# Both feed-forward products of a hybrid decoder step recast as seven block products, with the hidden activations passed through DRAM

## The reference

```python
x = x + mix
xn = rmsnorm(x, p['norm2_w'])
hid = jnp.square(jax.nn.relu(xn @ p['w_up']))     # 1024 -> 4096
x = x + hid @ p['w_down']                         # 4096 -> 1024
...
y = rmsnorm(x, final_norm_w)
```

## Time and profile before

| what | us |
|---|---|
| median of 3 runs | 2190.42 (2189.12 to 2192.53) |
| profiled execution, its span | 2187.7 |
| TensorE busy in the span | 2161.0 (99%) |
| VectorE, ScalarE, GpSimd busy | 972.0, 758.3, 570.4 |

### The profile page before, as it was taken

How to read it: one execution, slowest core, us unless ns; L and a number is a source line. 1 busy time by engine, 2 the same in 40 slices (tenths; PEclk the granted TensorE clock), 3 DMA queues, 4 the chain that set the end, 5 groups by cost and what they waited for, 6 DMA issues and landing times.

```text
span 2187.7 us, 36227 instructions
## 1 busy us (share of the span) xinstructions
PE 2161.0 (99%) x13766; PEld 2100.4 (96%) x13766; DVE 972.0 (44%) x1524; ACT 758.3 (35%) x1344; POOL 570.4 (26%) x375
## 2 busy tenths in 40 slices
PE   7999999999999999999999999999999999999998
PEld 6999999999899999899998999999999999999998
DVE  5888332334666563244445466442222222222226
ACT  5556323233456463233332334241212213122132
POOL 2338623233121112212213222222121222212120
PEclk9999999999999999999999999999999999999999
DMA  4224546442244323446432743211111111111112
GB/s 171 71 84 132 170 128 178 140 123 83 80 127 144 121 78 126 140 145 192 146 117 62 242 158 138 98 29 59 30 58 38 43 54 32 58 34 53 53 39 89
DMA packets 191538, 222.09 MB, mean 102 GB/s; under 512 B 38670, under 2 KB 146226, under 8 KB 191334
## 3 DMA queue, kind: packets, MB, share of 16 engines
q1 hardware_dynamic: 164364, 179.81, 27.1%
q10 hardware_dynamic: 27098, 41.23, 5.3%
HBM read 162.22 MB, written 58.77 MB: 101 GB/s over the span
## 4 chain that ended last, share of the span: by engine, by line
PE 77%; issue 10%; POOL 5%; DVE 4%; DMA 2%; ACT 1%; SPq 1%; ACTq 0%; POOLq 0%; DVEq 0%
PE D L438 64%; POOL w_lo L418 2%; PE D L2854 2%; POOL b_t L744 1%; POOL b_u L741 1%; DVE u_x L552 1%; DMA w_raw<-in_w_half 1%; PE MM L1906 1%; DMA d_bc<-rowd 0%; PE MB L1990 0%; PE MM L878 0%; PE MB L2302 0%; PE D L2397 0%; PE MB L2251 0%; PE MB L2270 0%
## 5 line engine op out<-in xcount | busy, mean ns | idle before, releaser
L438 PE MATMUL D<-xn_hi,w_hi 128*128 128x352 f32 x1992 | 661.9, 332 | 1.8 <-ACT u_in L513 1.0
L418 POOL TENSOR_TENSOR w_lo<-w_raw,w_hi 128x1024 fp32r<-128x1024 f32 (+1 forms) x163 | 339.1, 2080 | 1173.3 <-ACT w_hi L412 1173.3
L438 PE MATMUL D<-xn_lo,w_hi 128*128 128x352 f32 x1992 | 642.7, 323 | 0.0
L438 PE MATMUL D<-xn_hi,w_lo 128*128 128x352 f32 x1992 | 642.5, 323 | 0.0
L438 PEld LDWEIGHTS D<-xn_hi,w_hi 128*128 128x128 f32 x1992 | 374.5, 188 | 16.3 <-issue 12.8
L438 PEld LDWEIGHTS D<-xn_lo,w_hi 128*128 128x128 f32 x1992 | 374.5, 188 | 4.7 <-issue 3.8
L438 PEld LDWEIGHTS D<-xn_hi,w_lo 128*128 128x128 f32 x1992 | 374.3, 188 | 0.0
L412 ACT ACTIVATE w_hi<-w_raw 128x1024 fp32r<-128x1024 f32 (+1 forms) x163 | 143.8, 882 | 346.7 <-PE D L438 295.2
L438 PE MATMUL D<-z_lo,w_hi 128*128 128x352 f32 x768 | 247.9, 323 | 0.0
L438 PE MATMUL D<-z_hi,w_lo 128*128 128x352 f32 x768 | 247.8, 323 | 0.0
L438 PE MATMUL D<-z_hi,w_hi 128*128 128x352 f32 x768 | 247.3, 322 | 0.0
(11 more groups left out here) (565 smaller groups left out, 3063.6 us busy)
## 6 DMA issues: line engine op xcount, KB each, us to landing
w_raw<-in_w_proj SPq DMA_DIRECT2D x73, 512.0 KB, 3.9
proj<-stage ACTq DMA_DIRECT2D x60, 528.0 KB, 3.1
w_raw<-in_w_half SPq DMA_DIRECT2D x72, 256.0 KB, 2.6
w_raw<-in_w_full SPq DMA_DIRECT2D x24, 512.0 KB, 3.6
stage<-proj SPq DMA_DIRECT2D x23, 528.0 KB, 3.5
d_bc<-rowd SPq DMA_DIRECT2D x32, 256.0 KB, 5.6
m_in<-proj SPq DMA_DIRECT2D x32, 256.0 KB, 3.9
f_w<-in_w_full SPq DMA_DIRECT2D x16, 512.0 KB, 3.6
```

Source lines behind the costliest of these rows:

```text
L418: nc.gpsimd.tensor_tensor(w_lo[t.slot][:, 0:kt, :], raw(t)[0][:, 0:kt * P].rearrange("p (k m) -> p k m", m=P), w_hi[t.slot][:, 0:kt, :].bi ...
L438: last = nc.tensor.matmul(D[b][:, 0:GN], w[t.slot][:, k, :], x, start=(k == 0 and n == 0), stop=(k == kt - 1 and n == 2))
```

## The change

Both products are made in 2 x 2 blocks. For an up product the two halves of the output rows (a pair of tiles), the two halves of the inner dimension (even and odd k-tiles) and the two quarters of a column half (QW = 264) form the blocks; a scheme of 7 block products (i = 0 to 6) instead of 8 gives the four output blocks. A *round* is one pair of output tiles over a list of k-pairs `ks`. It has 7 products, each for both column halves n, each with 3 matmuls of 264 columns per k-pair. There are 16 up rounds over 4 k-pairs (2688 matmuls), then 20 down rounds (`DOWN_ROUNDS`) and 4 last ones (`LAST_ROUNDS`), together 64 k-pair steps (2688 matmuls).

Sums of weight blocks are made by GpSimd (4 per round, between 7 low parts), the high parts by ScalarE; a ring of 8 slots holds the parts, so the weights of product i of round s + 1 can be made once product i - 1 of round s is done. The seven classes of the input (3 plain blocks and 4 differences) are made for z in `out_proj` and for the hidden tiles in the down rounds listed in `PREPARED`, always one k-pair per round: ScalarE rounds, VectorE makes 7 low parts and 4 differences of 528 columns. `W_STEPS` below is GpSimd's order in a round: l is a low part, s a block sum that ScalarE's high part waits for.

Hidden tiles are stored to DRAM (`hd`) by SyncE after their squares, and loaded again for the down phase. Four tiles of `acc` are parked in DRAM (`resid`) meanwhile. All loops of this part are unrolled. Shortened to what the text behind speaks of:

```diff
-FB = 8
-FT = D_FF // P // FB
+QW = T // 4
+NCLS = 7
+UPS = D_FF // P // 2
+RING = 8
...
+        def room(pe, s, i, n):
+            s0, i0 = {0: (s - 2, 6), 1: (s - 1, 5), 2: (s, 0), 3: (s - 1, 3), 4: (s, 2), 5: (s, 1), 6: (s, 4)}[i]
+            if s0 >= 0:
+                pe.wait_ge(*(read_act if s0 < DOWN0 and i0 < 3 else read_dve)(s0, i0, n))
...
+        def product(pe, s, i, n):
+            up, pair, ks = ROUNDS[s]
+            pe.wait_ge(*w_made(s, f"l{i}"))
+            if up:
+                if s == 0:
+                    pe.wait_ge(*n2_dve.after(f"l{i}3"))
+            else:
+                pe.wait_ge(x_low, L_AT[ks[-1], i])
+            room(pe, s, i, n)
...
+            for k, kp in enumerate(ks):
+                xh, xl = x_hi[kp % 4][:, i, n, :], x_lo[kp % 4][:, i, n, :]
+                for j, (w, x) in enumerate(((hi, xh), (hi, xl), (lo, xh))):
+                    last = pe.matmul(to, w[:, k, :], x, start=fresh and k == 0 and j == 0, stop=k == len(ks) - 1 and j == 2, skip_group_check=True)
...
+        W_STEPS = ["l0", "s1", "l1", "s2", "l2", "s4", "l3", "s5", "l4", "l5", "l6"]
...
+        def w_high(act, s, i):
+            act.wait_ge(fw_ld[s % 2], 32 * (s // 2 + 1))
+            if i in (1, 2, 4, 5):
+                act.wait_ge(*w_made(s, f"s{i}"))
...
+        def up_copy(act, s, i):
+            for n in range(2):
+                act.wait_ge(*done(s, i, n))
+                if s:
+                    act.wait_ge(h_st[OUT_AT[i][0]][n], 16 * s)
+                elif i == 0:
+                    act.wait_ge(*n2_dve.after(f"a{KT - 1}"))
+                act.activation(hid(n, i), bank8(bank_of(s, i, n)), ACT.Copy).then_inc(f_act, 1)
...
+        def down_add(dve, s, i, n):
+            dve.wait_ge(*done(s, i, n))
+            dve.tensor_tensor(to, to, bank8(bank_of(s, i, n)), ALU.add).then_inc(f_dve, 1)
...
+        def feed_sp(sp):
+            w_load(sp, 0)
+            park(sp, 0)
+            w_load(sp, 1)
+            park(sp, 1)
+            for s in range(DOWN0):
+                if s >= 1:
+                    w_load(sp, s + 1)
+                if s == DOWN0 - 2:
+                    x_load(sp, 0)
+                    x_load(sp, 1)
+                for t in range(2):
+                    for n in range(2):
+                        sp.wait_ge(f_sq, 8 * s + 4 + 2 * t + n + 1)
+                        sp.dma_start(hd[2 * s + t, :, half(n)], stage[:, n, t * 2 * QW:(t + 1) * 2 * QW]).then_inc(h_st[t][n], 16)
+            for s in range(DOWN0, N_ROUNDS):
+                if s + 1 < N_ROUNDS:
+                    w_load(sp, s + 1)
+                if s == DOWN0:
+                    unpark(sp, 1)
+                    unpark(sp, 0)
+                for kp in X_LOADS.get(s - DOWN0, ()):
+                    x_load(sp, kp)
...
+        def feed_act(act):
...
+            for s in range(1, DOWN0):
+                for i in range(NCLS):
+                    if i < 3:
+                        up_copy(act, s, i)
+                    if i == 0:
+                        up_square(act, s - 1, NCLS - 1)
+                    if i >= 4:
+                        up_square(act, s, {4: 3, 5: 4, 6: 5}[i])
+                    if s == DOWN0 - 1:
+                        for kp in range(2):
+                            x_split_high(act, kp, i)
+                    w_high(act, s + 1, i)
+            up_square(act, DOWN0 - 1, NCLS - 1)
+            for s in range(DOWN0, LAST0):
+                for i in range(NCLS):
+                    if s - DOWN0 in PREPARED:
+                        x_split_high(act, PREPARED[s - DOWN0], i)
+                    w_high(act, s + 1, i)
...
+        def feed_dve(dve):
...
+            for s in range(DOWN0, LAST0):
+                for i in range(NCLS):
+                    for n in range(2):
+                        down_add(dve, s, i, n)
+                    if s - DOWN0 in PREPARED:
+                        x_split_low(dve, PREPARED[s - DOWN0], i)
```

More of the change, by code:

```diff
@@ new lines, in build @@
+        Round = namedtuple("Round", "up pair ks")
+        UP_ROUNDS = [Round(True, m, range(4)) for m in range(UPS)]
+        DOWN_ROUNDS = [Round(False, 1, range(0, 1)), Round(False, 2, range(0, 2))]
+        for first in range(0, 15, 3):
+            DOWN_ROUNDS += [Round(False, 0, range(first, first + 3)), Round(False, 3, range(first, first + 3))]
+            if first < 12:
+                DOWN_ROUNDS += [Round(False, 1, range(first + 1, first + 4)), Round(False, 2, range(first + 2, first + 5))]
@@ new lines, in build @@
+        X_AT = {x: k + 1 for k, x in enumerate(X_ORDER)}
+        X_STEPS = [step for kp, i in X_ORDER for step in [("low", kp, i)] + ([("difference", kp, NEXT_DIFFERENCE[i])] if i in NEXT_DIFFERENCE else [])]
+        L_AT = {(kp, i): k + 1 for k, (what, kp, i) in enumerate(X_STEPS) if what == "low"}
+        T_AT = {(kp, i): k + 1 for k, (what, kp, i) in enumerate(X_STEPS) if what == "difference"}
+        fw_ld = [sem(f"fw_ld{s}") for s in range(2)]
+        fw_high, fw_pool, fp_done = sem("fw_high"), sem("fw_pool"), sem("fp_done")
@@ new lines, in z_total, with z_roots @@
+        def z_total(pe):
+            pe.wait_ge(*n2_dve.after(f"a{KT - 1}"))
+            for lo, hi, b in SUM_COLS:
+                last = pe.matmul(bank8(b, hi - lo), ones, RS2[:, lo:hi], start=True, stop=True)
+            last.then_inc(*n2_pe.step("z"))
+        def z_roots(act):
+            act.wait_ge(*n2_pe.after("z"))
+            for g in (2, 0, 1):
+                lo, hi, b = SUM_COLS[g]
+                act.activation(RS2[:, lo:hi], bank8(b, hi - lo), ACT.Ln, bias=EPS, scale=1.0 / D_MODEL).then_inc(*n2_act.step(f"l{g}"))
+                act.wait_ge(*n2_act.after(f"l{g}"))
+                act.activation(RS2[:, lo:hi], RS2[:, lo:hi], ACT.Exp, scale=-0.5).then_inc(*n2_act.step(f"r{g}"))
@@ new lines, in feed_pe @@
+        def feed_pe(pe):
+            for s in range(LAST0):
+                for i in range(NCLS):
+                    for n in range(2):
+                        product(pe, s, i, n)
+                    if s == 0 and i == 2:
+                        z_total(pe)
+            for n in range(2):
+                for s in range(LAST0, N_ROUNDS):
+                    for i in range(NCLS):
+                        product(pe, s, i, n)
+                    if n and s == LAST0:
+                        last_total(pe, 0)
+            last_total(pe, 1)
@@ L3287 @@
     half = [tiles(wb[b], 4) for b in (HG, GD, ML)]
-    down = a["w_down"][0].reshape(FB, FT * P, D_MODEL)
-    half += [tiles(down[f], FT) for f in range(FB)]
     w_half = np.concatenate(half, 0)
```

728 lines of the change are left out of this document (462 added, 266 removed).

## The result

The changed kernel takes 2265.89 us (median of 4 runs, 2265.35 to 2266.86) against 2190.18 us (4 runs): ratio 1.0345, 95% interval 1.033 to 1.0359. It is slower by 3.4%, where 2197 (2150 to 2235) was forecast. The likeliest case had the sign, but the time lies outside the range. The profiled execution has a span of 2263.5 us against 2187.7.

A forecast was written before the change was run, and what follows sets the result against it. TensorE, busy in 99% of the span, was taken as the bound; -74.7 us for matmuls against added waits, start, handover and tail summed to +6.6, span 2194.3, forecast 2197 us, range 2150 to 2235.

The forecast's parts named there:

- The likeliest case: Whole kernel: the forecast itself, slower at 2197 us, own range 2180 to 2212, chance 0.40.
- the up rounds' term: 14 up rounds: late weight load delays ScalarE, GpSimd and the copy TensorE needs before product 4; +39 us (20 to 60).
- the loop: Up rounds: load, high parts with GpSimd's steps, squares, store and copies, without TensorE, take 23.5 us a round.
- The handover: Rounds 16 to 18: VectorE late, round 18's weights queued behind 4.3 MB; 39 us instead of 31, +8.5 (4 to 20).
- Start: Round 0 waits on input parts, copies and high parts, +10 us (6 to 16); VectorE and GpSimd in `out_proj`, +3.
- Last rounds: Rounds 21 to 23: GpSimd makes weights while TensorE needs them at once, +4.4; products with ones cost 1.4.
- B: Matmuls: 264 columns take 112.5 ns, only down and last rounds gain, 28 us, so 2169; chance 0.10.
- D: Matmuls: the distance stays 159.7 ns despite fewer columns, some 2360 us; chance 0.05.
- The matmuls' term: Feed-forward part: 5376 matmuls of 264 columns at 123 ns make 661.2 us, -74.7 us.
- prepared rounds: Down rounds: VectorE's two-SBUF-tile operations and GpSimd's exclude each other, TensorE waits 1.2 and 1.8 us; +12 us (0 to 45).
- rival C: Down phase: shared SBUF access sets the pace, 38 us instead of 12, so 2223; chance 0.20.
- Rival A: Up rounds: TensorE stays the bound because the load's landing hides, so 2158 us; chance 0.25.

The follow-up runs named there:

- experiment 2: Changed kernel with 24 matmuls whose result nobody reads added before product 4 of rounds 1 to 14; 2255.86 us, ratio 1.0293.
- experiment 9: Changed kernel, load still late, with ScalarE's copies of products 1 and 2 ahead of the next weights' high parts in rounds 1 to 14; 2249.76 us.
- experiment 5: On top of experiment 1: round 0's high parts ahead of the copies, three high parts of round 1 after that round's first copy; 2184.37 us.
- Experiment 3: Changed kernel with GpSimd's 11 operations in rounds 17 to 35 covering only the first 128 of 384 columns; 2248.72 us, ratio 1.026.
- experiment 1: Changed kernel with the up weights of round s + 2 loaded in round s, ahead of its stores; 2189.16 us, ratio 0.9994.
- experiment 10: Changed kernel with early loads and reordered start, handover and tail (2177.33 us), plus copies of products 1 and 2 ahead of high parts; 2201.45 us.

## Why the prediction was wrong, and where it was right

**The step that failed is the up rounds' term, +39, which measured +73.0.** The mechanism was the forecast one, a late load that comes round to TensorE through ScalarE and GpSimd. Two sizes in it were wrong. The first and larger is the loop. It was put at 23.5 us a round and takes 25.0 in experiment 2, where hardly a matmul runs at the lower clock, and 24.7 in experiment 9, where the waits stand elsewhere. Most of the difference lies between high part 5 and the next load: squares, stores, their landing, copies and squares again take 5.8 us for 4.6. The up rounds of experiment 2, its filler counted as waiting, come to 63.0 us of the 73.0, so 24 of the 34 us that the term is off are the loop's.

The second is an assumption that stood nowhere as a term: that a waiting TensorE goes on at the distance of 123 ns when the wait ends. The earlier trace rows show a clock of 1.00, but in a stretch without a pause, so they say nothing of a kernel with one. After ten of the 14 pauses matmuls ran at a clock of 0.50 for 3 to 6 us, which costs 1.5 to 2.6 us each. In these rounds it is 20.0 us on 51.9 of pauses, in the whole feed-forward part some 30. Experiment 2 shows the cause: with the pause filled, 1.5 of the 20.0 are left. It shows the price as well, the other 10 us, since a faster TensorE waits longer for the same loop. The Trainium skill describes this (TensorE: Matmul & The Clock Gate, "HAM oscillation — how this bites in real kernels"): a kernel whose matmuls wait for a transfer in each tile starts again at half clock each time. The trace agrees for ten of the 14 pauses, with 11 matmuls in 2 us for 18, and not for the other four. That section was the one to weigh against this change, and the prediction didn't.

**The handover, +8.5, measured +22.9**, over its upper bound of 20. The forecast counted the lag of VectorE and the queue, and both are there: SyncE's issues in order of time in the changed kernel, then ScalarE, VectorE and TensorE:

```profile
1870.60 0.94 SPq L2910 DMA_DIRECT2D raw<-in_w_dn  x2
1871.59 2.19 SPq L3181 DMA_DIRECT2D acc<-resid  x4
1874.02 1.52 SPq L3072 DMA_DIRECT2D f_rs<-hd  x2
...
1884.75 0.64 ACT L3080 ACTIVATE x_hi<-f_rs 128x528 fp32r<-128x528 f32 x1 [0.63 <-DMA f_rs<-hd]
...
1885.42 0.71 DVE L3085 TENSOR_TENSOR x_lo<-f_rs,x_hi 128x528 fp32r<-128x528 f32 x1 [5.88 <-ACT x_hi L3080]
...
1889.22 0.52 ACT L2924 ACTIVATE ring_hi<-w_raw 128x384 fp32r<-128x384 f32 x1 [3.83 <-DMA w_raw<-in_w_dn]
...
1893.29 0.56 PE L2984 MATMUL PB<-x_hi,w_hi 128*128 128x264 f32 x1 [9.06 <-DVE acc L3103]
```

The queue was longer than written: eight tiles of 528 KB are the 4.3 MB, and with round 18's two weight tiles of 384 KB it is 5.1. These weights land at 1889.2, which is 24.6 us after the start of round 16 instead of 21. What the forecast left out is who stands behind late weights. ScalarE is in order: between the high parts of the next weights stand the input parts of a later round. VectorE is in order too: the low part of such an input waits at its head, 5.88 us while ScalarE is at the weights of round 17 (and, for 0.6 us, at the hidden tile itself), then 2.75 more while it waits for those of round 18, and the additions that free TensorE's banks stand behind. So TensorE waits 9.06 us in round 17 for additions whose products had long been done, while the forecast looked for a wait on weights in round 18.

**Start, +13 with out_proj, measured +28.5.** Round 0 went nearly as written, with waits of 5.76 and 1.98 us for 5 and 2, and 1.9 for the product with ones instead of 1. Not foreseen were the wait of 4.43 in round 1, for ScalarE's copy of product 0 behind round 1's last high parts (experiment 5), and some 5 us at the lower clock, 3.4 here and 1.5 before the first product.

**Last rounds, +5.8, measured +13.5**: waits 6.5 for 4.4, products with ones 2.5 for 1.4, and 1.7 at the lower clock, to which it falls at 2214.9:

```profile
2214.00:2216.00 2.00, 1.82 (x9) 1.64 (x9) 1.09 (x3) 0.31 (x2) 1.94 (x4) 0.71 0.00 0
2216.00:2218.00 2.00, 2.00 (x11) 2.00 (x11) 0.52 (x2) 1.28 (x3) 1.71 (x3) 0.50 0.01 4
```

**Right** were these. The distance is 121.7 ns where 123 was taken, so rivals B and D are out. But it doesn't decide what the 13 ns left over are: the window of the earlier trace rows counts a matmul at each edge that lies in it only in part, and the starts of the kernel before are 160.3 ns apart, not 159.7. From there a surplus per matmul gives 123.6 ns, one that grows with the columns 120.2, and 121.7 lies between. The matmuls' term came out at -84.4 for -74.7, 7 us of it from 121.7 for 123 and 3 from 160.3 for 159.7. The Trainium skill's formula (TensorE: Matmul & The Clock Gate, "Back-to-back issue gap") would have 112.5 here; the section gives it for an isolated matmul and not for a stream with weight loads, and no row of this kernel shows it.

Every wait of rounds 2 to 14 was before product 4, released by ScalarE's copy, with ScalarE idle at a weight load some 6 us. In the first prepared rounds that come in threes the second had 1.2 us and the third 1.7 (1.2 and 1.8 forecast), and the term was +14.7 for +12, where four and a half turns of 3.0 would already be 13.5: the exclusion of VectorE's two-input operations and GpSimd's costs about that, not rival C's 38. Experiment 3 shows its cause. The Trainium skill's rule that the prediction quotes (SBUF — State Buffer, "Who interferes with whom") agrees with it. The tail is 22.4 for 20.5. Rival A, no waits in the up rounds, is what experiment 1 makes true by another order; its 2158 was too low, as the start, the handover and the last rounds cost more than forecast. A run is 1.8 to 2.0 us above its own span here, not 2.7, which changes nothing.

The bounds of three terms didn't hold: the up rounds (20 to 60), the start (6 to 16) and the handover (4 to 20). In all three the clock's cost comes on top of the waits, with the same sign. A range made of independent bounds (2150 to 2235) can't hold that.

## What to carry to other kernels

When a change puts a pause into a stream of matmuls that had none, price it twice: the wait, and the matmuls at 1.2 GHz that may follow it (here 20.0 us on top of 51.9, of which filling the pause won 10). When a loop of several engines sets the pace, add up all of its links, the way back through stores and copies too: 1.5 us too little in a round was some 20 us here. Before a change is given up, look at the order of issues in the queues: moving one load a round ahead was worth 76.7 us here, nearly as much as the fewer columns had saved (84.4). Moving a step ahead in one engine's order moves others back, though, and these have to be priced as well (experiment 10: 24 us). An engine that works in order passes a late transfer on to everything behind it, so ask at each wait on data what else is queued there.

## What the runs showed of the hardware

- Pauses alike in length have different prices. Of the 14 in the up rounds of the changed kernel the seven of 3.9 us or more were all followed by a lower clock. Of the seven from 2.9 to 3.4 us those that ended at 1550.69, 1574.62, 1649.46 and 1806.35 cost nothing more, those at 1525.27, 1624.41 and 1781.44 1.5 to 1.6 us each. In the last rounds the clock fell at 2214.9, behind six pauses of 0.3 to 1.0 us within 7 us, and the slow matmuls cost 1.7 us; a single one of 1.6 us that ended at 1980.90 cost nothing. What sets it was not tried.
- A filler of matmuls without use made the kernel faster (experiment 2, 10 us), as the clock stayed up.
- TensorE's distance between matmuls, each with its own weights, is 121.7 ns at 264 columns and 160.3 at 352: 11.7 and 13.6 ns above the columns' time at 2.4 GHz.
- The exclusion shows in one operation's duration: VectorE's subtraction of two tiles of 528 columns takes 0.71 us alone, and had a median of 1.40 beside GpSimd's operations of 384 columns and 0.78 (for the other half of the tiles 0.85) beside those of 128. Its addition with one operand in PSUM stayed at 0.42 throughout.
